# Turning the last group's probabilities on VectorE, and walking three column blocks of the output product side by side

## The chip, the cores and the metric

The kernel runs on one core of one Trainium2 chip. The metric is the device time of one execution in microseconds (us), as the median of the runs. Engines are named as in the profile: PE is TensorE's matmuls and PEld its weight loads, DVE is VectorE, ACT is ScalarE, POOL is GpSimd, SP is SyncE (here it only issues transfers).

## What is computed

Two layers on x (256 rows, 2048 columns, fp32). Each is x + rms_norm(mixer(rms_norm(x))). The change is in layer 0, whose mixer is attention:

```
proj = hn @ w_in                       # 256x2048 @ 2048x8192 -> q, k, v, z
q, k = rope(q), rope(k)                # 16 heads of 128
p = softmax(causal(q @ k.T * scale))   # one block of 256 keys: plain causal attention
y = ((p @ v) * silu(z)) @ w_out        # 256x2048 @ 2048x2048
```

Layer 1 is a gated depthwise convolution with a product on either side (w_in1, w_out1). Nothing in it is touched.

## The kernel before

**The large products.** Every product of 256 rows with a weight matrix is done in column blocks of 512 and slices of two k tiles of 128 (SL_K = 2, SLICES = 8 slices for K = 2048). fp32 accuracy comes from splitting both operands into a high and a low part in fp32r and adding three products: `slice_products` (L419) issues for each slice 2 k tiles x 2 row tiles x 3 parts = 12 matmuls of 128x128 with 128x512 (L429 to L431) into `acc[:, par, m]`. PSUM has eight banks: `acc` is two halves (par) of two banks (m = 0, 1), and `X[0]` to `X[3]` are four single banks for everything else.

**The weights' pipeline.** SyncE loads 1 MB (four k tiles, two slices) into one of four `raw` buffers (`load`, L299), and may do so when the low parts of the slices that were there before are made (`lo_ready`). ScalarE rounds a slice to its high part (`high`, L766, instruction L781) into one of four slots (RING = 4); for slice s it waits until TensorE has done slice s - 4 (`w_used`). VectorE subtracts to get the low part (`low`, L1057, instruction L1066), and TensorE waits for that (`lo_ready`) ahead of slice s. Each engine walks the same numbering of slices, and small work is put behind chosen slices of its own loop: `if s == ...` after `high(s)`, `low(s)` or `slice_products(s)`.

**Attention.** The first product (S_QKVZ) goes over four groups (G = 4 heads, 512 columns of q, k, v and z each; 32 slices a group). Behind slice 26 of a group TensorE makes the scores into `X[0..3]`; VectorE takes maxima and ScalarE exponentials (`exponentials`, L881), which end in `probs` (128 x 4 x 384: for each head three 128x128 blocks) and count `p_ready`. For the product with v the probabilities must be turned into `pT`.
- For groups 0 to 2 this happens in the next group's loop (`group_end`, L1186): VectorE turns 32x32 blocks from `probs` to `pT`, four instructions of 32x384 (`turn_probs`, L1165, instruction L1168) behind each of slices 2, 3, 4 and 5 (TURN_P = 2); TensorE multiplies with v behind slice 4 (`values`, L565; VALUES_AT = 4) into X[0] and X[1]; VectorE gates behind slice 7 (`gate_outputs`, L1132), turns the result behind slices 8 to 11 (`turn_heads`, L1179), and splits it behind 13 (`heads_low`, L1147), ScalarE making the high part behind its slice 13 (`heads_high`, L866).
- The last group's end lies in the output product's loop. There TensorE itself turns the probabilities behind slice 0: twelve transposes of 128x128 into X (`probs_T`, L559, instruction L562); VectorE copies them to `pT` behind slice 1 (`last_group_end`, L1198, instruction L1202), TensorE multiplies with v behind slice 1, and gating, turning and splitting follow behind slices 4, 5 to 8 and 10.

**The output product of layer 0** (S_OUT0, 32 slices, loop at L607). `OUT0_ORDER` (L76) names for every slice its column block n and its k slice. The last group's heads are k slices 6 and 7, and they are the last to be ready. So the order is block 0 slices 0 to 5, block 1 slices 0 to 5, then (0,6), (0,7), (1,6), (1,7), then blocks 2 and 3 whole. Block n accumulates in acc half n % 2. `ulo_ready` (L612) is the wait of TensorE for the split heads; `acc_free` (L451) is its wait, at a block's first slice, for the half to have been read.

**Emptying a block.** `OUT0_LAST` (L78) is the last slice of each block. Behind slices 17, 19 and 27 of their own loops ScalarE takes the squares of the rows of a block (`out0_squares`, L919; instruction L818, two instructions) and VectorE multiplies them with the gains to `y0` (`out0_rows`, L1247; instruction L1254, two instructions, counting `acc_read`). The gains `gpost0` are a 1 MB broadcast (L360), issued after the fourth load of the output weights, when TensorE has finished the last slice of the first product. The last four slices (28 to 31) are done for row tile 0 and then for row tile 1, and the next product's input is prepared between them.

Of the kernel before, what the change touches and what calls it, by code (L numbers as in the profile page):

```python
# [23 lines left out]
P = 128  # L24
# [50 lines left out]
SILU_AT = (1, 6)  # L75
OUT0_ORDER = tuple([(0, i) for i in range(6)] + [(1, i) for i in range(6)] + [(0, 6), (0, 7), (1, 6), (1, 7)]  # L76
                   + [(n, i) for n in (2, 3) for i in range(SLICES)])
OUT0_LAST = (13, 15, 23, 31)  # L78
TURN_Q, TURN_K = 15, 24
# [5 lines left out]
def build(nc, x, pre_g, post_g, w_in0, w_out0, w_in1, b_in, w_dw, b_dw, ln_g, ln_b, w_out1, b_out,  # L85
# [5 lines left out]
    with ctx:  # L91
# [126 lines left out]
        p_ready = sem("p_ready")  # L218
        pT_done = sem("pT_done")
        pT_ready = sem("pT_ready")  # L220
# [33 lines left out]
        row1_done = sem("row1_done")  # L254
        stored = sem("stored")

        block = ctx.enter_context(nc.Block())
# [148 lines left out]
        def _(pe):  # L406
# [11 lines left out]

            def slice_products(first, it, per, s, hi, lo, place=None):  # L419
                slot = s % RING  # L420
                block_no, part = place or (s // SLICES, s % SLICES)
                par = (first // SLICES + block_no) % 2
                pe.wait_ge(lo_ready[slot], rounds(first, it, per, s))
                order = [(i, m) for i in range(SL_K) for m in range(MT)]
                for n, (i, m) in enumerate(order):
                    k = SL_K * part + i
                    rows = slice(m * P, (m + 1) * P)
                    a = acc[:, par, m]
                    nc.tensor.matmul(a, hi[:, k, rows], w_hi[:, slot, i], start=(k == 0), stop=False)  # L429
                    nc.tensor.matmul(a, hi[:, k, rows], w_lo[:, slot, i], start=False, stop=False)  # L430
                    last = nc.tensor.matmul(a, lo[:, k, rows], w_hi[:, slot, i], start=False,  # L431
                                            stop=(k == KT - 1))
                last.then_inc(w_used[slot], 1)
# [124 lines left out]

            def probs_T(g, h):  # L559
                pe.wait_ge(p_ready, G * g + h + 1)  # L560
                for i in range(3):
                    last = nc.tensor.transpose(X[h][:, i * P:(i + 1) * P], probs[:, h, i * P:(i + 1) * P], ident[:])  # L562
                last.then_inc(pT_done, 1)

            def values(g):  # L565
# [41 lines left out]
            for s in range(4 * SLICES):  # L607
                n, part = OUT0_ORDER[s]
                if part == 0:
                    acc_free(16 + n)  # L610
                if n == 0 and part % 2 == 0:
                    pe.wait_ge(ulo_ready, part // 2 + 1)  # L612
                if s < 4 * SLICES - RING:
                    slice_products(S_OUT0, 0, 0, s, uT_hi, uT_lo, (n, part))
                if s == 0:
                    for h in range(G):
                        probs_T(NG - 1, h)
                if s == 1:
                    values(NG - 1)
# [145 lines left out]
        def _(act):  # L765
# [105 lines left out]

            def group_end(s, g, last=False):

                if s == 3:
                    if not (isinstance(g, int) and g == 0):
                        act.wait_ge(u_ready, g)
                    block_rows(S_QKVZ, g, 32, 31, z_row, rms[0], ACT.Silu)
                if s == (10 if last else SPLIT_U):
                    heads_high(g)
# [39 lines left out]
            def out0_squares(n):  # L919

                for m in range(MT):
                    if n == NG - 1 and m == 0:
                        act.wait_ge(row0_done, 1)
                    else:
                        act.wait_ge(w_used[OUT0_LAST[n] % RING], rounds(S_OUT0, 0, 0, OUT0_LAST[n]))
                    squares(junk1[:], acc[:, n % 2, m], m, n, 8 + MT * n + m)
                    if n == NG - 1 and m == 0:
# [5 lines left out]
            for s in range(4 * SLICES):  # L933
                high(S_OUT0, 0, 0, s)
                group_end(s, NG - 1, True)
                if s in (17, 19, 27):
                    out0_squares((17, 19, 27).index(s))
                if s > 4 * SLICES - RING:
# [117 lines left out]
        def _(dve):  # L1056
# [140 lines left out]

            def last_group_end(s):  # L1198
                if s == 1:
                    for h in range(G):  # L1200
                        dve.wait_ge(pT_done, h + 1)
                        nc.vector.tensor_copy(pT[:, h], X[h][:, 0:3 * P]).then_inc(pT_ready, 1)  # L1202
                    inverse_sums(NG - 1)
                if s == 4:
                    gate_outputs(NG - 1)
                if s in range(5, 9):
                    turn_heads(s - 5, NG - 1)
                if s == 10:
                    heads_low(NG - 1)

            def maxima(g, h):
# [35 lines left out]
            def out0_rows(n, ms=(0, 1)):  # L1247
# [3 lines left out]
                for m in ms:  # L1251
                    dve.wait_ge(ssq_ready, 8 + MT * n + m + 1)
                    c = slice(n * NCOL, (n + 1) * NCOL)
                    last = nc.vector.tensor_tensor(y0[:, m, c], acc[:, n % 2, m], gpost0[:, c], ALU.mult)  # L1254
                    if m == 1:
                        last.then_inc(acc_read, 1)

            for s in range(4 * SLICES):
                low(S_OUT0, 0, 0, s)
                last_group_end(s)  # L1260
                if s in (17, 19, 27):
                    out0_rows((17, 19, 27).index(s))
                if s > 4 * SLICES - RING:
# [339 lines left out]
```

## Time and profile before

| | |
|---|---|
| median of 3 runs | 845.37 us (845.22 to 845.59) |
| the profiled execution's own time | 845.41 us |
| span of the profiled execution | 843.6 us |
| mean granted TensorE clock | 0.998 |
| TensorE matmul busy | 833.9 us, 3851 instructions |
| VectorE busy | 703.9 us |
| ScalarE busy | 428.2 us |
| GpSimd busy | 341.2 us |

The span is from the first to the last instruction; the execution's time has 1.8 us around it. Times in the rows below are microseconds from the span's start, durations in us or ns as the row says. A matmul is shown from its start to its modelled end, and neighbours overlap: what one costs is the distance from its start to the next one's. A weight load (PEld) stands ahead of its matmul.

### The profile page before, as it was taken

The page shows a single profiled execution, that of the slowest core. Times are in us where ns is not written, and L with a number is a line of the kernel's source. Part 1 is how long each engine was busy: PE and PEld are TensorE (multiplying, and loading weights), DVE is VectorE, ACT ScalarE, POOL GpSimd, SP SyncE. Part 2 cuts the span into 40 slices and gives each one's busy share as a digit, 9 for nine tenths or more (in the row PEclk, how much of TensorE's full clock was granted, in tenths as well). Part 3 has the DMA queues.
Part 4 walks back from the last instruction along what each step waited for, and adds up shares of the span by engine and source line. Part 5 has one row for each costly group of instructions (what it writes and reads, how often), then busy time and mean ns, then how long its engine had stood idle before and what let it go on. Part 6 is the DMA issues. An engine that isn't in the chain of part 4 may idle for free.

```text
span 843.6 us, 12102 instructions
## 1 busy us (share of the span) xinstructions
PE 833.9 (99%) x3851; PEld 691.6 (82%) x3851; DVE 703.9 (83%) x1222; ACT 428.2 (51%) x592; POOL 341.2 (40%) x171
## 2 busy tenths in 40 slices
PE   9999999999999999999999999999999999999996
PEld 6888888888888888888888788888888888888884
DVE  5688799988999899968556629999999999998655
ACT  6744534464444635454445675445445464574541
POOL 0342005500540014400000298888888878894000
PEclk9999999999999999999999999999999999999999
DMA  9956556656567556646655466555555646566522
GB/s 316 315 169 206 175 157 193 198 158 197 156 188 220 177 149 183 215 149 223 216 186 192 133 200 200 176 176 197 188 167 193 198 151 200 194 219 244 192 99 100
DMA packets 97510, 159.50 MB, mean 189 GB/s; under 512 B 3300, under 2 KB 38468, under 8 KB 97092
## 3 DMA queue, kind: packets, MB, share of 16 engines
q1 hardware_dynamic: 97428, 159.04, 58.7%
q8 instruction: 20, 0.33, 0.2%
q14 instruction: 14, 0.11, 0.0%
q10 hardware_dynamic: 48, 0.02, 0.0%
HBM read 156.94 MB, written 2.10 MB: 189 GB/s over the span
## 4 chain that ended last, share of the span: by engine, by line
PE 98%; issue 1%; DMA 0%; DVE 0%; ACT 0%; DVEq 0%; POOLq 0%; POOL 0%; SPq 0%
PE acc L429 29%; PE acc L431 29%; PE acc L430 29%; PE X L439 1%; PE acc L414 1%; PE acc L416 1%; PE acc L415 1%; PE acc L495 1%; PE acc L510 1%; DMA xrow<-in_x 0%; PE X L571 0%; PE X L556 0%; PE X L555 0%; PE X L572 0%; PE X L570 0%
## 5 line engine op out<-in xcount | busy, mean ns | idle before, releaser
L781 ACT ACTIVATE w_hi<-raw 128x1024 fp32r<-128x1024 f32 x282 | 298.7, 1061 | 345.6 <-PE acc L431 345.0
L429 PE MATMUL acc<-w_hi,xT_hi 128*128 128x512 f32 x864 | 338.7, 392 | 0.0
L431 PE MATMUL acc<-w_hi,xT_lo 128*128 128x512 f32 x864 | 336.4, 389 | 0.0
L430 PE MATMUL acc<-w_lo,xT_hi 128*128 128x512 f32 x864 | 336.2, 389 | 0.0
L1066 DVE TENSOR_TENSOR w_lo<-raw,w_hi 128x1024 fp32r<-128x1024 f32 x180 | 242.1, 1362 | 72.3 <-ACT w_hi L781 70.0
L1550 POOL TENSOR_TENSOR w_lo<-raw,w_hi 128x1024 fp32r<-128x1024 f32 x102 | 248.0, 2438 | 48.8 <-ACT w_hi L781 48.4
L431 PEld LDWEIGHTS acc<-w_hi,xT_lo 128*128 128x128 f32 x864 | 162.2, 188 | 33.9
L429 PEld LDWEIGHTS acc<-w_hi,xT_hi 128*128 128x128 f32 x864 | 162.3, 188 | 33.2 <-DVE xT_lo L1085 0.3
L430 PEld LDWEIGHTS acc<-w_lo,xT_hi 128*128 128x128 f32 x864 | 162.3, 188 | 32.9
L1350 DVE SCALAR_TENSOR_TENSOR X<-u_pad,taps,X 128x256 f32<-128x256 f32 x464 | 182.6, 484 | 0.0
L1513 POOL TENSOR_TENSOR small<-small 128x1 f32<-128x1 f32 (+1 forms) x7 | 4.3, 617 | 222.9 <-DVE small L1296 124.2
L1527 POOL TENSOR_TENSOR rope_t<-q_row,sin_t 128x256 f32<-128x256 f32 x16 | 15.3, 988 | 178.8 <-ACT q_row L789 178.8
L429 PE MATMUL acc<-w_hi,uT_hi 128*128 128x512 f32 x112 | 43.8, 391 | 0.0
L429 PE MATMUL acc<-w_hi,vT_hi 128*128 128x512 f32 x112 | 43.7, 391 | 0.0
L431 PE MATMUL acc<-w_hi,vT_lo 128*128 128x512 f32 x112 | 43.6, 389 | 0.0
L431 PE MATMUL acc<-w_hi,uT_lo 128*128 128x512 f32 x112 | 43.6, 389 | 0.0
L430 PE MATMUL acc<-w_lo,vT_hi 128*128 128x512 f32 x112 | 43.6, 389 | 0.0
L430 PE MATMUL acc<-w_lo,uT_hi 128*128 128x512 f32 x112 | 43.6, 389 | 0.0
L1527 POOL TENSOR_TENSOR rope_t<-k_row,sin_t 128x256 f32<-128x256 f32 x16 | 16.2, 1042 | 44.3 <-ACT k_row L789 44.3
L1158 DVE STREAM_TRANSPOSE qT<-q_row 32x256 f32<-32x256 f32 x64 | 27.9, 436 | 1.0
L1158 DVE STREAM_TRANSPOSE kT<-k_row 32x256 f32<-32x256 f32 x64 | 27.9, 436 | 1.0
L1158 DVE STREAM_TRANSPOSE uT<-u_row 32x256 f32<-32x256 f32 x64 | 27.9, 436 | 1.0
(153 smaller groups left out, 770.7 us busy)
## 6 DMA issues: line engine op xcount, KB each, us to landing
raw<-in_w_in SPq DMA_DIRECT2D x78, 1024.0 KB, 5.3
raw<-in_w_in SPq DMA_DIRECT2D x66, 512.0 KB, 4.4
raw<-in_w_out SPq DMA_DIRECT2D x32, 1024.0 KB, 5.0
gpost<-in_post_g SPq DMA_DIRECT2D x2, 1024.0 KB, 6.4
xrow<-in_x SPq DMA_DIRECT2D x4, 256.0 KB, 5.8
raw<-in_w_in SPq DMA_DIRECT2D x4, 256.0 KB, 4.8
xrow<-in_x SPq DMA_DIRECT2D x2, 512.0 KB, 9.9
bout<-in_b_out SPq DMA_DIRECT2D x1, 1024.0 KB, 10.2
```

The costliest lines, as they stand in the source:

```text
L414: nc.tensor.matmul(a, hi[:, k, rows], wh[:, i], start=(k == 0), stop=False)
L415: nc.tensor.matmul(a, hi[:, k, rows], wl[:, i], start=False, stop=False)
L416: last = nc.tensor.matmul(a, lo[:, k, rows], wh[:, i], start=False, stop=(k == KT - 1))
L429: nc.tensor.matmul(a, hi[:, k, rows], w_hi[:, slot, i], start=(k == 0), stop=False)
L430: nc.tensor.matmul(a, hi[:, k, rows], w_lo[:, slot, i], start=False, stop=False)
L431: last = nc.tensor.matmul(a, lo[:, k, rows], w_hi[:, slot, i], start=False, stop=(k == KT - 1))
L781: nc.scalar.activation(w_hi[:, slot], raw[:, u % LOADS, 2 * half:2 * half + 2], ACT.Copy).then_inc(hi_ready[slot], 1)
L1066: nc.vector.tensor_tensor(lo_of(first, it, s), raw[:, u % LOADS, 2 * half:2 * half + 2], hi_of(first, it, s).bitcast(f32), ALU.subtract).t ...
L1158: last = nc.vector.transpose(dst[b * BLK:(b + 1) * BLK].rearrange("p h (m c) -> p m h c", m=MT) [:, :, :, a * BLK:(a + 1) * BLK], row[a * ...
L1350: ins = nc.vector.scalar_tensor_tensor(out=out_, in0=u, scalar=taps[:, bass.ds(tile + k * KT, 1)], in1=part, op0=ALU.mult, op1=ALU.add)
L1527: last = nc.gpsimd.tensor_tensor(t[:, :, o], v[:, :, w], sin_t[:, m:m + 1, o].to_broadcast([P, G, HALF]), ALU.mult)
L1550: nc.gpsimd.tensor_tensor(w_lo[:, slot], raw[:, u % LOADS, 2 * half:2 * half + 2], w_hi[:, slot].bitcast(f32), ALU.subtract).then_inc(lo_r ...
```

## The change

The last group is treated like the others: `probs_T`, its semaphore and `last_group_end` go, VectorE runs `group_end` in the output product's loop too, and TensorE multiplies with v behind slice 4. The last group's heads are so ready later, and the order of the output product is changed: three blocks go over k slices 0 to 5 (slices 0 to 17), then the same three over k slices 6 and 7 (slices 18 to 23), then block 3 whole (24 to 31). Three blocks open at a time need a third pair of banks: block 2 accumulates in X[2] and X[3] (`out0_bank`), and its first slice (12) waits for `p_ready` in place of `acc_free`. Blocks 0, 1 and 2 are emptied behind slices 23, 25 and 27.

```diff
--- before.py
+++ after.py
@@ -73,9 +73,10 @@
 OUT1_POOL = 10
 FINAL_AT = (0, 4, 8, 10)
 SILU_AT = (1, 6)
-OUT0_ORDER = tuple([(0, i) for i in range(6)] + [(1, i) for i in range(6)] + [(0, 6), (0, 7), (1, 6), (1, 7)]
-                   + [(n, i) for n in (2, 3) for i in range(SLICES)])
-OUT0_LAST = (13, 15, 23, 31)
+OUT0_ORDER = tuple([(n, i) for n in (0, 1, 2) for i in range(6)] + [(n, i) for n in (0, 1, 2) for i in (6, 7)]
+                   + [(3, i) for i in range(SLICES)])
+OUT0_LAST = (19, 21, 23, 31)
+OUT0_EVICT = (23, 25, 27)
 TURN_Q, TURN_K = 15, 24
 SCORES_AT = 26
 TURN_P, VALUES_AT, GATE_ROWS_AT, TURN_U, SPLIT_U = 2, 4, 7, 8, 13
@@ -216,7 +217,6 @@
         max_ready = sem("max_ready")
         negmax_ready = sem("negmax_ready")
         p_ready = sem("p_ready")
-        pT_done = sem("pT_done")
         pT_ready = sem("pT_ready")
         inv_ready = sem("inv_ready")
         pv_done = sem("pv_done")
@@ -254,6 +254,10 @@
         row1_done = sem("row1_done")
         stored = sem("stored")
 
+        def out0_bank(n, m):
+
+            return X[2 + m][:] if n == 2 else acc[:, n % 2, m]
+
         block = ctx.enter_context(nc.Block())
 
         def cols(w):
@@ -416,7 +420,7 @@
                     last = nc.tensor.matmul(a, lo[:, k, rows], wh[:, i], start=False, stop=(k == KT - 1))
                 return last
 
-            def slice_products(first, it, per, s, hi, lo, place=None):
+            def slice_products(first, it, per, s, hi, lo, place=None, banks=None):
                 slot = s % RING
                 block_no, part = place or (s // SLICES, s % SLICES)
                 par = (first // SLICES + block_no) % 2
@@ -425,7 +429,7 @@
                 for n, (i, m) in enumerate(order):
                     k = SL_K * part + i
                     rows = slice(m * P, (m + 1) * P)
-                    a = acc[:, par, m]
+                    a = banks[m][:] if banks else acc[:, par, m]
                     nc.tensor.matmul(a, hi[:, k, rows], w_hi[:, slot, i], start=(k == 0), stop=False)
                     nc.tensor.matmul(a, hi[:, k, rows], w_lo[:, slot, i], start=False, stop=False)
                     last = nc.tensor.matmul(a, lo[:, k, rows], w_hi[:, slot, i], start=False,
@@ -555,12 +559,6 @@
                 nc.tensor.matmul(s[:, 0:P], qT[:, h, 0:P], kT[:, h, 0:P], start=True, stop=True)
                 nc.tensor.matmul(s[:, 2 * P:3 * P], qT[:, h, P:SEQ], kT[:, h, P:SEQ], start=True, stop=True
                                  ).then_inc(s_done, 1)
-
-            def probs_T(g, h):
-                pe.wait_ge(p_ready, G * g + h + 1)
-                for i in range(3):
-                    last = nc.tensor.transpose(X[h][:, i * P:(i + 1) * P], probs[:, h, i * P:(i + 1) * P], ident[:])
-                last.then_inc(pT_done, 1)
 
             def values(g):
                 pe.wait_ge(pT_ready, G * (g + 1))
@@ -606,16 +604,15 @@
 
             for s in range(4 * SLICES):
                 n, part = OUT0_ORDER[s]
-                if part == 0:
+                if part == 0 and n == 2:
+                    pe.wait_ge(p_ready, G * NG)
+                elif part == 0:
                     acc_free(16 + n)
                 if n == 0 and part % 2 == 0:
                     pe.wait_ge(ulo_ready, part // 2 + 1)
                 if s < 4 * SLICES - RING:
-                    slice_products(S_OUT0, 0, 0, s, uT_hi, uT_lo, (n, part))
-                if s == 0:
-                    for h in range(G):
-                        probs_T(NG - 1, h)
-                if s == 1:
+                    slice_products(S_OUT0, 0, 0, s, uT_hi, uT_lo, (n, part), X[2:4] if n == 2 else None)
+                if s == VALUES_AT:
                     values(NG - 1)
 
             last_slices = range(4 * SLICES - RING, 4 * SLICES)
@@ -869,13 +866,13 @@
                     last = nc.scalar.activation(uT_hi[:, bass.ds(g * 4 + 2 * b, 2)], uT[:, 2 * b:2 * b + 2], ACT.Copy)
                 last.then_inc(uhi_ready, 1)
 
-            def group_end(s, g, last=False):
+            def group_end(s, g):
 
                 if s == 3:
                     if not (isinstance(g, int) and g == 0):
                         act.wait_ge(u_ready, g)
                     block_rows(S_QKVZ, g, 32, 31, z_row, rms[0], ACT.Silu)
-                if s == (10 if last else SPLIT_U):
+                if s == SPLIT_U:
                     heads_high(g)
 
             def exponentials(g, h, first):
@@ -923,7 +920,7 @@
                         act.wait_ge(row0_done, 1)
                     else:
                         act.wait_ge(w_used[OUT0_LAST[n] % RING], rounds(S_OUT0, 0, 0, OUT0_LAST[n]))
-                    squares(junk1[:], acc[:, n % 2, m], m, n, 8 + MT * n + m)
+                    squares(junk1[:], out0_bank(n, m), m, n, 8 + MT * n + m)
                     if n == NG - 1 and m == 0:
                         row_high(0, 0)
                         row_high(1, 0)
@@ -932,9 +929,9 @@
 
             for s in range(4 * SLICES):
                 high(S_OUT0, 0, 0, s)
-                group_end(s, NG - 1, True)
-                if s in (17, 19, 27):
-                    out0_squares((17, 19, 27).index(s))
+                group_end(s, NG - 1)
+                if s in OUT0_EVICT:
+                    out0_squares(OUT0_EVICT.index(s))
                 if s > 4 * SLICES - RING:
                     high(S_AG, 0, 16, s - (4 * SLICES - RING + 1))
             high(S_AG, 0, 16, RING - 1)
@@ -1195,19 +1192,6 @@
                 if s == SPLIT_U:
                     heads_low(g)
 
-            def last_group_end(s):
-                if s == 1:
-                    for h in range(G):
-                        dve.wait_ge(pT_done, h + 1)
-                        nc.vector.tensor_copy(pT[:, h], X[h][:, 0:3 * P]).then_inc(pT_ready, 1)
-                    inverse_sums(NG - 1)
-                if s == 4:
-                    gate_outputs(NG - 1)
-                if s in range(5, 9):
-                    turn_heads(s - 5, NG - 1)
-                if s == 10:
-                    heads_low(NG - 1)
-
             def maxima(g, h):
                 dve.wait_ge(s_done, G * g + h + 1)
 
@@ -1251,15 +1235,15 @@
                 for m in ms:
                     dve.wait_ge(ssq_ready, 8 + MT * n + m + 1)
                     c = slice(n * NCOL, (n + 1) * NCOL)
-                    last = nc.vector.tensor_tensor(y0[:, m, c], acc[:, n % 2, m], gpost0[:, c], ALU.mult)
+                    last = nc.vector.tensor_tensor(y0[:, m, c], out0_bank(n, m), gpost0[:, c], ALU.mult)
                     if m == 1:
                         last.then_inc(acc_read, 1)
 
             for s in range(4 * SLICES):
                 low(S_OUT0, 0, 0, s)
-                last_group_end(s)
-                if s in (17, 19, 27):
-                    out0_rows((17, 19, 27).index(s))
+                group_end(s, NG - 1)
+                if s in OUT0_EVICT:
+                    out0_rows(OUT0_EVICT.index(s))
                 if s > 4 * SLICES - RING:
                     low(S_AG, 0, 16, s - (4 * SLICES - RING + 1))
             low(S_AG, 0, 16, RING - 1)
```

## Rows read from the trace of the kernel before

**Rows 1.** The page, busy time by engine.
```profile
PE 833.9 (99%) x3851; PEld 691.6 (82%) x3851; DVE 703.9 (83%) x1222; ACT 428.2 (51%) x592; POOL 341.2 (40%) x171
```
**Rows 2.** Waits of TensorE, whole span: us in total, times, longest.
```profile
PE acc L537 <- POOL small L1508: 1.0, 1, 1.0
PE X L476 <- DMA xrow<-in_x: 0.3, 1, 0.3
```
**Rows 3.** Timeline of PE, output product's first seven slices: start, us, engine, line, operation.
```profile
378.61 0.39 PE L429 MATMUL acc<-w_hi,uT_hi 128*128 128x512 f32 x1
...
381.33 1.47 PE L562 MATMUL X<-ident,probs 128*128 128x128 f32 x12
382.56 0.48 PE L429 MATMUL acc<-w_hi,uT_hi 128*128 128x512 f32 x1
382.87 0.40 PE L430 MATMUL acc<-w_lo,uT_hi 128*128 128x512 f32 x1
...
385.41 0.38 PE L570 MATMUL X<-v_row,pT 128*128 128x128 f32 x2
...
396.27 0.39 PE L429 MATMUL acc<-w_hi,uT_hi 128*128 128x512 f32 x1
...
398.99 0.39 PE L429 MATMUL acc<-w_hi,uT_hi 128*128 128x512 f32 x1
```
**Rows 4.** Timeline of PE, the last group's own start: slices 0, 5 and 6.
```profile
286.18 0.39 PE L429 MATMUL acc<-w_hi,xT_hi 128*128 128x512 f32 x1
...
302.38 0.48 PE L429 MATMUL acc<-w_hi,xT_hi 128*128 128x512 f32 x1
...
305.19 0.39 PE L429 MATMUL acc<-w_hi,xT_hi 128*128 128x512 f32 x1
```
**Rows 5.** Timelines of DVE and PEld at that border, then at the first.
```profile
284.81 1.23 DVE L1066 TENSOR_TENSOR w_lo<-raw,w_hi 128x1024 fp32r<-128x1024 f32 x1 [1.49 <-ACT w_hi L781]
...
288.36 1.23 DVE L1066 TENSOR_TENSOR w_lo<-raw,w_hi 128x1024 fp32r<-128x1024 f32 x1
...
291.96 1.23 DVE L1066 TENSOR_TENSOR w_lo<-raw,w_hi 128x1024 fp32r<-128x1024 f32 x1
...
296.82 2.33 DVE L1168 STREAM_TRANSPOSE pT<-probs 32x384 f32<-32x384 f32 x4
...
299.56 0.41 PEld L570 LDWEIGHTS X<-v_row,pT 128*128 128x128 f32 x2
...
111.97 2.33 DVE L1168 STREAM_TRANSPOSE pT<-probs 32x384 f32<-32x384 f32 x4
...
114.70 0.41 PEld L570 LDWEIGHTS X<-v_row,pT 128*128 128x128 f32 x2
```
**Rows 6.** Both kinds of turning by source line: ns min/median/max, first and last start.
```profile
L562 PE MATMUL X<-ident,probs x12: 270/272/273, 381.3 to 382.5; 128*128 128x128 f32 x12
L1168 DVE STREAM_TRANSPOSE pT<-probs x48: 514/570/574, 101.2 to 298.6; 32x384 f32<-32x384 f32 x48
```
**Rows 7.** Stretches: length; busy by engine PE, PEld, DVE, ACT, POOL; PEclk, DMA share, GB/s.
```profile
381.33:385.41 4.08, 4.08 (x25) 3.57 (x24) 3.55 (x7) 2.12 (x3) 0.00 (x0) 1.00 0.98 388
286.18:302.38 16.20, 16.20 (x86) 13.86 (x84) 14.99 (x21) 8.80 (x9) 0.00 (x0) 1.00 0.57 176
```
**Rows 8.** Timelines of ACT, SP and DVE around the start of the output product.
```profile
372.15 0.20 ACT L887 ACTIVATION_READ_ACCUMULATOR probs<-X,small 128x1 f32 x1
...
378.80 0.34 SPq L360 DMA_DIRECT2D gpost<-in_post_g  x1
...
381.86 1.95 DVE L1202 COPY pT<-X 128x384 f32<-128x384 f32 x4 [6.12 <-PE X L562]
...
383.83 3.45 DVE L1066 TENSOR_TENSOR w_lo<-raw,w_hi 128x1024 fp32r<-128x1024 f32 x3
```
**Rows 9.** Timelines of DVE and PE: the first block read, and slice 16.
```profile
423.24 1.28 DVE L1254 TENSOR_TENSOR y<-acc,gpost 128x512 f32<-128x512 f32 x2
...
426.19 0.39 PE L429 MATMUL acc<-w_hi,uT_hi 128*128 128x512 f32 x1
```

## The prediction

> **What bounds the kernel now.** I read the page first: TensorE is busy for 99% of the span [rows 1], and the chain of waits below it on the page runs through TensorE nearly throughout. So a change is worth what it does to TensorE's stream, unless it makes TensorE wait. The list of waits says the same more sharply: in the whole span TensorE waited for another engine twice, for 1.0 and 0.3 us, both in the first microseconds [rows 2]. Busy time alone is not enough, since matmuls overlap; I therefore went on to the timeline, where the cost of an instruction is the distance between the starts of its neighbours. A slice of the weights is twelve matmuls, and one slice to the next is 2.72 us (396.27 to 398.99 [rows 3]), so 0.2267 us per matmul although each is shown as 0.39 us long.
>
> The place of the change is the start of the first output product, at 378.61 [rows 3]. There the reader should see two interruptions: twelve transposes of the probabilities behind slice 0, and the products with the values behind slice 1. The other three groups of heads have the same work in the other form, turned by VectorE, and the values behind slice 4; the border between the third and the last group is the model for what the changed kernel will do [rows 4, 5].
>
> **The twelve transposes go.** Their mean is 272 ns [rows 6], but they lie in each other: the first starts at 381.33 and the next product at 382.56, so the path holds 1.23 us for them, 0.103 us each. Behind them slice 1 runs from 382.56 to 385.41, 2.85 us in place of 2.72: 0.13 us more, of which 0.08 is the first matmul (next start after 0.31, not 0.23) and the rest small excesses in the same slice [rows 3]. Sum: 1.23 + 0.13 = 1.36 us. A second way to the same number: the first slice's start to the sixth slice's start holds five slices and the values at either border. It is 378.61 to 396.27 = 17.66 with transposes and values after slice 1 [rows 3]. At the model border 286.18 to 302.38 is 16.20, up to the restart after the values, whose own excess then falls into the next slice (302.38 to 305.19, 2.81, so 0.09) [rows 4]. 17.66 - 16.20 - 0.09 = 1.37. I take 1.36. The ends: 1.23 if the slow slice has another cause (it lay under transfers that kept the queues 98% busy [rows 7]), and 1.37.
>
> **A rule on the price of a transpose.** The trace shows 272 ns as duration and 0.103 us as distance. The Trainium skill (TensorE: Matmul & The Clock Gate, Part 4: PE-mode transpose) gives about 275 ns for a 128x128 transpose in a kernel's context; the duration in the trace agrees, and by the rule taken as a price per transpose the saving would be more than twice as large.
>
> **The copies go, turns come.** VectorE loses four copies (1.95 us from 381.86 [rows 8]) and the 6.12 us that it waited for TensorE before them. It gains sixteen block transposes, four per slice over slices 2 to 5, 2.33 us for the last four at the model border [rows 5], 16 x 0.57 = 9.1 us in all by the median of one [rows 6]; so it is some 7.2 us busier. Nothing of this lies on TensorE's path as long as the last turn ends before the values need it. That is the one new wait that can matter, and I price it from the model: VectorE works there without a pause from 284.81 to 299.15 (four splits, a reciprocal, sixteen turns; 14.34 us), and TensorE loads the first turned block at 299.56 [rows 5]. The cover is 0.41 us. At the border of the first two groups it is the same: 111.97 + 2.33 = 114.30 against 114.70 [rows 5]. Slice 0 starts at 378.61, which is 92.43 us after 286.18 [rows 3, 4], and what ScalarE does for slices 2 to 5 is the same at both borders, so the chain should run from 377.24 to 391.58 and the values start their load at 391.99. The probabilities themselves are finished at 372.15 + 0.20 = 372.35 [rows 8], long before. Cost: 0, with 0.41 us in hand; behind a late turn TensorE would simply stand, with slice 5 queued behind the values.
>
> Could the turns be slower here than in the model? The one thing that is different is traffic: the 1 MB broadcast of the gains is issued at 378.80, and the queues are 98% busy from 381.33 to 385.41, against 57% at the model border [rows 7, 8]. Three splits inside that traffic took 3.45 us, 1.15 each, no more than the 1.23 of the model border [rows 5, 8]. So I take nothing. The Trainium skill (SBUF, State Buffer; section SBUF: two separate sides) says that a transfer and a compute operation cannot slow each other there; by this the reserve stays whole, and the splits under traffic agree.
>
> The Trainium skill (VectorE: DVE Perf Modes, Rules for kernel authors) also speaks against the change: for a 128x128 transpose it recommends TensorE. By cost per engine the trace agrees, 9.1 us on VectorE against 1.23 on TensorE, but what counts here is which engine has time to spare.
>
> **Gate, turning and splitting of the last heads move later** (slices 7, 8 to 11 and 13 instead of 4, 5 to 8 and 10; ScalarE's part from 10 to 13). TensorE needs the result for the last four row tiles, now first in slice 18 instead of slice 12. By the model's spacing slice 18 starts near 378.61 + 2.60 + 18 x 2.72 + 0.1 = 430.3. The heads' split follows slice 13's low part, whose high part waits for slice 9, done near 408.5; three VectorE steps of some 3 us later it is there, near 415. Cost 0, about 15 us in hand. The loads of the weights keep their sizes and number, only their addresses swap; SyncE's queue waits for the low parts, which come at the model's times. Cost 0.
>
> **The third block in two other banks.** Ninety-six matmuls write X2 and X3 in place of acc. No row has this form; from above I bound it by the excess of a restart, 0.08 us [rows 3], at each of the four changes of block, 0.3 us. A gain is excluded, since the pitch is 0.2267 us in every block already. Nearest are the alternating banks m = 0 and 1 inside a slice, which cost nothing: 0. Its wait for p_ready is long met in slice 12.
>
> **Emptying the blocks** moves from slices 17, 19, 27 to 23, 25, 27; the first two keep their distance of four slices behind the block's last product. What is new: block 3 reuses the second half of acc in slice 24, two slices after the second block ends in slice 21. Before, the first block had the same distance (last product in slice 13, next use in slice 16): read by 423.24 + 1.28 = 424.52, needed at 426.19, 1.67 us in hand [rows 9]. Cost 0. Behind a late reading slice 24 and all the rest would stand.
>
> **Sum.** -1.36 us. The profiled execution took 845.41 us around a span of 843.6 and is 0.04 above the median of 845.37. So 845.41 - 1.36 = 844.05 for it, span 842.2, and 844.0 for the median: 0.16% less. A measurement of this kernel can tell about 0.2%, 1.69 us, from no change, so the likeliest outcome counts as no change though the direction is down.
>
> **Rivals.**
> First, the transposes cost their whole duration: 12 x 0.272 = 3.26 us, so 842.1, faster. For it: 272 ns in the row [rows 6]. Against it: 1.23 us between their neighbours [rows 3]. Chance 0.04. (This is what the page's 275 ns would give.) With 0.08 for a smaller surplus, over 0.33 us beyond my sum, from restarts that I have missed: faster 0.12.
> Second, the turns come somewhat late, by 0.4 to 1.7 us, and eat the gain: around 844.9. Against: three borders of groups, and no wait at any [rows 2]. Chance 0.07, counted as no change.
> Third, ending slower: the same wait, but one whole step of VectorE (split and turn, 3.60 us, 288.36 to 291.96 [rows 5]) later. TensorE stands 3.60 - 0.41 = 3.19 us in front of the values, net +1.83, 847.2. It decides once the last turn is over 0.41 + 1.36 + 1.69 = 3.46 us late. For it: the thin cover and a chain without a pause. Against: the same alignment as the model, and splits that do not slow under traffic. Chance 0.05.
> Fourth, the second block is read a slice late: 2.72 - 1.67 = 1.05 us lost in front of slice 24, 845.1, no change. Chance 0.02.
> That leaves 0.74 for the forecast itself, and no change in all 0.83.
>
> **Range.** The forecast's own spread is 843.7 to 844.4 (terms 1.23 to 1.37, 0.3 for the banks, and 0.2 for the scatter of the runs). Towards the late turns I go to 845.1, and below to 843.5 for part of the surplus. What is outside is the whole-duration case, the slower one and the tails.
>
> **What would show it.** The row of transposes and copies is gone; 64 block turns of the probabilities instead of 48; no interruption behind slice 0; the values' load about 13.4 us after the start of slice 0; TensorE's waits still only two; five slices with values 16.2 us. Wrong: a wait of TensorE for the turns or for the reading of acc, or a pitch over 0.227 us in the third block.

## The result, and the profile after

| | before | changed |
|---|---|---|
| median | 845.37 us | 848.46 us (846.68 to 848.79, 7 runs) |
| profiled execution | 845.41 us | 846.72 us |
| its span | 843.6 us | 844.9 us |

The ratio over all runs is 1.0027, 95% interval [1.0017, 1.0037]: 0.27% slower, where 844.0 and no measurable change were forecast. The seven runs fall into two heaps, three at 846.68 to 847.26 with a mean granted clock of 0.997 and four at 848.46 to 848.79 with 0.995. The median lies in the upper heap, so the medians are further apart, 3.1 us or 0.37%; the profiled execution is of the lower heap.

At the place of the change everything went as forecast. The timeline of PE in the changed kernel, at the first slice, at the values and at the sixth slice:

```profile
378.48 0.39 PE L433 MATMUL acc<-w_hi,uT_hi 128*128 128x512 f32 x1
...
392.08 0.38 PE L568 MATMUL X<-v_row,pT 128*128 128x128 f32 x2
...
394.68 0.48 PE L433 MATMUL acc<-w_hi,uT_hi 128*128 128x512 f32 x1
```

Slice 0 to slice 5 is 394.68 - 378.48 = 16.20 us, as at the model border [rows 4], against 17.66 before [rows 3]. The last turn and the load of the first turned block, from the timelines of DVE and PEld:

```profile
389.13 2.33 DVE L1165 STREAM_TRANSPOSE pT<-probs 32x384 f32<-32x384 f32 x4
...
391.86 0.41 PEld L568 LDWEIGHTS X<-v_row,pT 128*128 128x128 f32 x2
```

389.13 + 2.33 = 391.46, so 0.40 us in hand; 0.41 was forecast. The loss lies some 350 us further on. The waits of TensorE in the changed kernel, which answer to [rows 2]:

```profile
PE acc L433 <- issue: 2.1, 1, 2.1
PE acc L541 <- POOL small L1492: 1.0, 1, 1.0
PE X L706 <- POOL small L1497: 0.4, 1, 0.4
```

Two are new. The big one is ahead of the last product of layer 1 (`vT_hi`). The profile puts it down to "issue", but the program has TensorE wait there for the low part of `vT`, which VectorE makes. The small one (L706) is ahead of the matmuls that spread the statistics of the convolution's rows, some 20 us earlier, and these start from sums that VectorE makes too. The profile's chain tells whose lateness it is:

```profile
PE 70%; DVE 16%; issue 9%; DVEq 3%; ACT 1%; DMA 0%; POOL 0%; POOLq 0%; SPq 0%; ACTq 0%
PE acc L433 20%; PE acc L435 20%; PE acc L434 20%; DVE X L1334 12%; DVEq L1333 2%; DVE u_pad L1345 2%; PE acc L418 1%; PE acc L420 1%; PE acc L419 1%; PE X L433 1%; PE X L435 1%; PE X L434 1%; PE acc L514 1%; PE acc L499 1%; PE X L443 1%
```

VectorE had 0% of this chain before, and TensorE 98%. L1334 are the convolution's taps and L1345 is the gate of a pair of its input tiles (u_pad times sigmoid). VectorE walks eight pairs, each with one gate and 62 taps, from the first sigmoid to the statistics that the last product needs. Timelines around the start of the last product, first of the kernel before and then of the changed one:

```profile
743.70 3.42 DVE L1424 TENSOR_TENSOR vT_lo<-cT,vT_hi 128x1024 fp32r<-128x1024 f32 x1
...
746.96 0.39 PE L431 MATMUL acc<-w_hi,xT_lo 128*128 128x512 f32 x1
747.23 0.47 PE L429 MATMUL acc<-w_hi,vT_hi 128*128 128x512 f32 x1
```

```profile
745.07 3.40 DVE L1408 TENSOR_TENSOR vT_lo<-cT,vT_hi 128x1024 fp32r<-128x1024 f32 x1
...
746.11 0.39 PE L435 MATMUL acc<-w_hi,xT_lo 128*128 128x512 f32 x1
748.57 0.47 PE L433 MATMUL acc<-w_hi,vT_hi 128*128 128x512 f32 x1 [2.07 <-issue]
```

Before, VectorE's low part ended at 743.70 + 3.42 = 747.12 and TensorE started at 747.23, 0.04 us behind its usual pitch: both chains arrived together, and nothing of this wait was long enough to be listed. Afterwards TensorE is there 0.85 us earlier (746.11) and VectorE 1.35 us later (748.47). The distance to the next start is 2.46 us (746.11 to 748.57) where it was 0.27, so 2.19 more. The sum is -0.85 + 2.19 = +1.34 us, the 1.3 us between the spans. Ahead of the statistics TensorE had been 1.46 us early (728.25 against 729.71); the other 0.61 us went into the small wait.

VectorE starts the convolution 1.47 us earlier (the first gates below) and comes out of it 2.37 us later. The first instruction behind it, from the timelines of DVE before and after:

```profile
716.57 3.66 DVE L1378 BATCH_NORM_STATS2 small<-c_row 128x6 f32<-128x512 f32 x6
```

```profile
718.94 3.65 DVE L1362 BATCH_NORM_STATS2 small<-c_row 128x6 f32<-128x512 f32 x6
```

The loop is thus 3.84 us longer. Up to the last product 1.0 of the 2.37 us are made good: before, VectorE had waited 0.38 us for TensorE on the way, and one of its products (L1413, now L1397) had taken 3.03 us in place of 2.40. Where the convolution loses its time is seen in the eight gates. Timeline of DVE, the first four gates before:

```profile
505.94 0.69 DVE L1361 TENSOR_TENSOR u_pad<-u_pad,sig  x1 [10.96 <-ACT sig L983]
...
531.82 0.69 DVE L1361 TENSOR_TENSOR u_pad<-u_pad,sig  x1 [0.26 <-issue]
...
557.49 2.64 DVE L1361 TENSOR_TENSOR u_pad<-u_pad,sig  x1 [0.23 <-issue]
...
585.11 0.69 DVE L1361 TENSOR_TENSOR u_pad<-u_pad,sig  x1 [0.23 <-issue]
```

and after:

```profile
504.47 0.69 DVE L1345 TENSOR_TENSOR u_pad<-u_pad,sig  x1 [10.94 <-ACT sig L980]
...
530.47 2.85 DVE L1345 TENSOR_TENSOR u_pad<-u_pad,sig  x1 [0.28 <-issue]
...
558.34 0.69 DVE L1345 TENSOR_TENSOR u_pad<-u_pad,sig  x1 [0.27 <-issue]
...
584.05 2.77 DVE L1345 TENSOR_TENSOR u_pad<-u_pad,sig  x1 [0.27 <-issue]
```

A gate takes 0.69 us or up to 2.9 us, and the eight are 0.69, 0.69, 2.64, 0.69, 2.90, 0.69, 0.69, 1.74 before (10.73 us) and 0.69, 2.85, 0.69, 2.77, 0.69, 2.78, 1.28, 2.63 after (14.38 us): 3.65 us more, out of the 3.84. In this stretch GpSimd splits the weights, 2.40 us in each 2.72, so that a gate nearly always meets a split. The splits nearest to the second gate, before and then after:

```profile
531.84 7.84 POOL L1550 TENSOR_TENSOR w_lo<-raw,w_hi 128x1024 fp32r<-128x1024 f32 x3 [0.32 <-ACT w_hi L781]
```

```profile
530.37 2.40 POOL L1534 TENSOR_TENSOR w_lo<-raw,w_hi 128x1024 fp32r<-128x1024 f32 x1 [0.31 <-ACT w_hi L778]
```

Before, the gate (531.82) starts 0.02 us ahead of the split and is undisturbed. After, it starts (530.47) 0.10 us behind the split and ends at 533.32, 0.55 us after the split's end. My theory (A): a gate that starts behind a split of GpSimd waits for its end, and a few hundredths of a microsecond decide which of the two is first; from then on all later gates fall otherwise. The Trainium skill (SBUF, State Buffer; section SBUF: two separate sides) describes it: a VectorE operation with two SBUF inputs and a GpSimd operation that reads SBUF need a shared pair of ports, whoever starts first has it for the whole instruction, "the other fully blocks". The gate has two SBUF inputs, and both traces agree in both directions. The eight gates in them that start while a split runs all end 0.55 us behind that split's end. A split that starts while a gate runs is lengthened in its turn; beside the sixth gate of the kernel before (638.67 to 639.36) it takes 2.78 us in place of 2.40:

```profile
638.84 2.78 POOL L1550 TENSOR_TENSOR w_lo<-raw,w_hi 128x1024 fp32r<-128x1024 f32 x1 [0.39 <-ACT w_hi L781]
```

The rivals: (B) the loss comes from the output product's new order or its banks; (C) VectorE's convolution loop is slower apart from its gates (by the two profiles it is, but only by 0.19 us); (D) it is TensorE's earlier arrival that sets how gates and splits meet.

### The profile page after: what moved, and what is told of

Its sections match the earlier page's. It is cut to its first block, busy times and chain, and to the rows that moved or that the text cites. A ratio compares the mean times of both kernels' runs of the same rounds, so it can differ in the third digit from the quotient of the medians.

```text
span 844.9 us, 12090 instructions
## 1 busy us (share of the span) xinstructions
PE 833.0 (99%) x3839; PEld 690.1 (82%) x3839; DVE 714.0 (85%) x1234; ACT 428.0 (51%) x592; POOL 341.3 (40%) x171
## 4 chain that ended last, share of the span: by engine, by line
PE 70%; DVE 16%; issue 9%; DVEq 3%; ACT 1%; DMA 0%; POOL 0%; POOLq 0%; SPq 0%; ACTq 0%
PE acc L433 20%; PE acc L435 20%; PE acc L434 20%; DVE X L1334 12%; DVEq L1333 2%; DVE u_pad L1345 2%; PE acc L418 1%; PE acc L420 1%; PE acc L419 1%; PE X L433 1%; PE X L435 1%; PE X L434 1%; PE acc L514 1%; PE acc L499 1%; PE X L443 1%
## 5 line engine op out<-in xcount | busy, mean ns | idle before, releaser
L1334 DVE SCALAR_TENSOR_TENSOR X<-u_pad,taps,X 128x256 f32<-128x256 f32 x464 | 182.7, 482 | 0.0
L1165 DVE STREAM_TRANSPOSE pT<-probs 32x384 f32<-32x384 f32 x64 | 36.3, 567 | 1.0
L433 PE MATMUL acc<-w_hi,uT_hi 128*128 128x512 f32 x80 | 31.2, 390 | 0.0
L434 PE MATMUL acc<-w_lo,uT_hi 128*128 128x512 f32 x80 | 31.1, 389 | 0.0
L435 PE MATMUL acc<-w_hi,uT_lo 128*128 128x512 f32 x80 | 31.1, 389 | 0.0
```

Source lines behind the costliest of these rows:

```text
L1165: last = nc.vector.transpose(pT[b * BLK:(b + 1) * BLK].rearrange("p h (i c) -> p (h i) c", i=3) [:, :, a * BLK:(a + 1) * BLK], probs[a * B ...
L1334: ins = nc.vector.scalar_tensor_tensor(out=out_, in0=u, scalar=taps[:, bass.ds(tile + k * KT, 1)], in1=part, op0=ALU.mult, op1=ALU.add)
```

## Experiments

The number that a measured time is set against is the median of the kernel before in the same comparison. Unless said otherwise, the outputs are computed in full.

**The sigmoid in a PSUM bank, loop unrolled.** X[3] is free during the convolution and X[1] between its transposes; the gate then has one SBUF input.

```diff
-last = nc.scalar.activation(sig[:, buf, c], X[1][...], ACT.Sigmoid, ...)
+last = nc.scalar.activation(X[3 - 2 * buf][...], X[1][...], ACT.Sigmoid, ...)
-with dve.Fori(0, SLICES) as h:
-    nc.vector.tensor_tensor(pair, pair, sig[:, bass.ds(h % 2, 1)]..., ALU.mult)
+with dve.Fori(0, SLICES // 2) as q:
+    for b in (0, 1):
+        h = q * 2 + b
+        nc.vector.tensor_tensor(pair, pair, X[3 - 2 * b]..., ALU.mult)
# and TensorE waits for gate h - 1 before it writes X[1] for an even pair h
```

On the changed kernel:

> The changed kernel, but ScalarE puts the sigmoid into a PSUM bank (X[3] for even, X[1] for odd pairs), so that VectorE's gate of the convolution input has one SBUF input instead of two. Theory A (the gates were held up by GpSimd's low-part splits): all eight gates take about 0.7 us, the end of the convolution on VectorE comes 8 to 9 us earlier, TensorE does not wait ahead of the last product, and the local saving of 1.36 us is seen in full: 844.0. Theory B (the loss is in the output product's new order, the third pair of banks or the emptying): the loss stays, 846.5 to 848.5. Theory C (VectorE's convolution loop itself is slower in the changed kernel, gates aside): most of the loss stays, over 846.

On the kernel before:

> The same edit on the kernel before. Theory A: its gates lose about 5 us of delay too, but TensorE waited there by 0.1 us at most, so the median stays near 845.3, and the difference to the changed kernel with this edit is the 1.36 us of the transposes. Theories B and C: near 845.3 as well, with the changed kernel above it.

Measured: 849.11 us and 850.2 us against 845.06, ratios 1.0044 [1.0031, 1.0058] and 1.0048 [1.0034, 1.0062]. Both forecasts missed, by the time. The timeline of DVE of the first shows why; gates 2 to 4:

```profile
530.67 0.68 DVE L1350 TENSOR_TENSOR u_pad<-u_pad,X 128x512 f32 x1
...
559.30 0.69 DVE L1350 TENSOR_TENSOR u_pad<-u_pad,X 128x512 f32 x1 [2.98 <-issue]
...
585.00 0.68 DVE L1350 TENSOR_TENSOR u_pad<-u_pad,X 128x512 f32 x1
```

All eight gates are 0.68 or 0.69 us, as theory A has it. But at each of the three turns of the now twice as long loop VectorE stands for 2.98, 2.83 and 4.42 us with nothing to wait for in the program, and TensorE waits 3.2 us for the sixth gate. So the edit had a cost of its own, and this pair decides nothing about the total. I took the length of the loop's body as the cause of the pauses, and tested that below.

**A nudge of 0.1 us, on the kernel before.**

```diff
+if first:
+    nc.scalar.activation(small[:, 120:121], rms[2][:, 0:1], ACT.Copy)   # one column, not used
 for c in range(2):
     nc.scalar.activation(u_pad[...], X[0][...], ACT.Identity, ...)
```

> The kernel before with one ScalarE copy of one column ahead of the very first sigmoid, so that VectorE's convolution starts some 0.1 to 0.3 us later against GpSimd's splits and nothing else changes. Theory A: the second gate, which in the kernel before starts 0.02 us ahead of a split, now starts behind it and takes over 2 us; other gates fall differently too, TensorE waits ahead of the last product and the median is 1 to 3 us above before, about 847. Theories B and C: at most 0.3 us above before, 845.4 to 845.7.

Measured: 849.4 us (848.11 to 849.75) against 845.06, ratio 1.0047 [1.0033, 1.0061]. From the transposes ahead of it to the first gate it is 4.61 us (501.16 to 505.77) instead of 4.51 (501.43 to 505.94). The second gate and the split beside it:

```profile
531.65 2.87 DVE L1363 TENSOR_TENSOR u_pad<-u_pad,sig  x1 [0.26 <-issue]
```

```profile
531.57 2.40 POOL L1552 TENSOR_TENSOR w_lo<-raw,w_hi 128x1024 fp32r<-128x1024 f32 x1 [0.32 <-ACT w_hi L781]
```

0.10 us more, and the gate is 0.08 us behind the split. The eight gates are then those of the changed kernel within 0.1 us (2.87, 2.85, 2.87, 1.30 and 2.69 in the same places), and TensorE waits 2.0 us for VectorE. This is theory A in the kernel before, with nothing of the change in it; B and C allow 0.3 us. The size was larger than the 1 to 3 us that I gave: the profiled execution, 848.11, is 3.05 us above, and the median 4.3. What lies between these two no trace of this run shows.

**TensorE's twelve transposes put back into the changed kernel**, result not used:

```diff
+if s == 0:
+    pe.wait_ge(p_ready, G * NG)
+    for h in range(G):
+        for i in range(3):
+            nc.tensor.transpose(X[h][:, i * P:(i + 1) * P], probs[:, h, i * P:(i + 1) * P], ident[:])
```

> The changed kernel with the twelve TensorE transposes of the probabilities put back behind slice 0 (their result is not used). All the rest is as changed. Theory A with the program's layout or a small delay on VectorE deciding the race, not TensorE's earlier arrival: the gates are held up as in the changed kernel and the time is 1.2 to 1.5 us above it, 848 to 850. Theory D (it is TensorE's earlier arrival by 1.36 us that sets the phase): the gates fall as in the kernel before and the time is 845.4.

Measured: 849.14 us against 845.06. The gates are 0.69, 2.86, 0.69, 2.77, 0.69, 2.78, 1.27, 2.63, as in the changed kernel. D falls: with TensorE's work as before, VectorE is still late. Here the profile caught something more. Stretches of this kernel: the wait ahead of the last product, the ten matmuls behind it, and the next ones:

```profile
747.10:749.50 2.40, 0.38 (x2) 0.00 (x0) 2.37 (x2) 2.40 (x5) 1.49 (x2) 1.00 0.02 7
749.53:753.26 3.73, 3.73 (x10) 2.91 (x11) 3.51 (x9) 1.75 (x3) 3.73 (x2) 0.54 0.78 279
753.30:757.00 3.70, 3.70 (x20) 3.06 (x19) 3.67 (x3) 2.08 (x3) 2.35 (x2) 1.00 0.45 127
```

(length; busy by PE, PEld, DVE, ACT, POOL; PEclk, DMA share, GB/s.) After the wait of about 2 us the granted clock is 0.54, so nearly all of the stretch is at 1.2 GHz instead of 2.4; the tenth start behind it comes 3.75 us after the first instead of 2.12, which is 1.6 us. In the changed kernel's profile the same wait did not bring the clock down (the matmuls behind 748.57 keep their pitch). That fits the two heaps of its runs, 2.0 us apart with mean clocks of 0.997 and 0.995. Of the changed kernel itself no slower run was profiled. The nearest is the changed kernel with six idle instructions (below, profiled at 848.63 us and 0.995), whose gates are the same to 0.01 us. Behind its wait the granted clock is down too, with matmuls 0.43 us apart, again 1.6 us in all:

```profile
748.85:752.30 3.45, 3.45 (x10) 2.68 (x11) 3.33 (x8) 1.73 (x3) 3.45 (x2) 0.59 0.96 300
```

So the upper heap is most likely the lower one with this half clock added, 1.6 of the 2.0 us.

**The sigmoid in a bank, loop not unrolled.** X[0] to X[3] become slices of one PSUM tensor XX, so that the gate can choose its bank by an index; the loop body keeps its length.

```diff
+X = [XX[:, i] for i in (2, 1, 3, 0)]
-nc.vector.tensor_tensor(pair, pair, sig[:, bass.ds(h % 2, 1)]..., ALU.mult)
+nc.vector.tensor_tensor(pair, pair, XX[:, bass.ds(h % 2, 1)]..., ALU.mult)
# ScalarE's sigmoid and TensorE's two waits for the gates as in the first edit
```

> The changed kernel with the sigmoid in a PSUM bank and the gate with one SBUF input, but VectorE's loop over the pairs not unrolled this time: the bank is chosen by an index, so the loop body is as long as in the changed kernel. Theory A (gates held up by GpSimd's splits): no gate over 0.75 us, no pause of 2.6 to 4.4 us at the loop's turn, the convolution ends 8 us earlier than in the changed kernel (near 708 instead of 716.6), TensorE does not wait ahead of the last product: 844.0. If the pauses of the unrolled loop had another cause than its length (the bank, the waits of TensorE), they stay and the time is over 848.

> The same edit on the kernel before. Theory A: 845.3, no more than 0.1 us of TensorE's waits to gain, and 1.36 us above the changed kernel with the edit. Otherwise over 848.

Measured against 845.28: the changed kernel with it 844.37 us, ratio 0.9989 [0.998, 0.9998]; the kernel before with it 845.54, ratio 1.0003 [0.9994, 1.0012]. Two lines of the first's timeline of DVE:

```profile
684.75 0.69 DVE L1349 TENSOR_TENSOR u_pad<-u_pad,X  x1 [0.27 <-issue]
...
722.82 1.30 DVE L1366 BATCH_NORM_STATS2 small<-X 128x6 f32<-128x512 f32 x2 [5.44 <-PE X L701]
```

The last gate begins at 684.75 (691.64 in the changed kernel), all eight take 0.69 us, no turn of the loop over 0.28, and VectorE now waits 5.44 us for TensorE ahead of the last statistics. It comes out of the convolution at 710.11, 8.8 us earlier than in the changed kernel (the "708 instead of 716.6" of my expectation used the time of the kernel before for the comparison). TensorE's wait ahead of the last product is gone. So: with the collisions away the changed kernel is 1.17 us faster than the kernel before with the same edit, where 1.36 was forecast. By the two ratios it is 1.2 us, and their intervals just overlap, so this size is rough. It is also 4.1 us below the changed kernel's own median, from another comparison. The pauses of the unrolled loop went with its length, while the bank and TensorE's new waits stayed.

**The two parts apart, both with the gate in a bank.** Order, banks and emptying alone (turning as before, by TensorE):

> With the gate in a bank, so that the convolution does not cover what is measured: the new order, the third pair of banks and the later emptying alone; the probabilities are turned by TensorE and copied by VectorE as before. Theory A: this part costs and brings nothing, 845.3. Theory B (order or banks cost): above 845.6.

Turning alone (the output product's old order, `OUT0_EVICT` 17, 19, 27):

> With the gate in a bank: VectorE turns the probabilities, but the output product keeps the order of the kernel before, so that TensorE needs the last group's split heads in slice 12. In the changed kernel's trace they are there at 412.8 and slice 12 starts at 413.8, so TensorE should just not wait: 844.0 if it holds, up to 845.0 if the split is late by a microsecond.

Measured against 845.28: order alone 845.24 us, ratio 1.0004 [0.9995, 1.0013]; turning alone 843.95 us, ratio 0.9985 [0.9976, 0.9994]. B falls. TensorE waits nowhere in the output product in either. Turning alone has the lowest median of the study, clear of the kernel before, but the 0.4 us to the whole change with the gate in a bank are within the noise. The split heads are in time for slice 12, so the third pair of banks is not needed.

**What made the gate late: the length of VectorE's program.** In the changed kernel the first round of the loop is 26.00 us (504.47 to 530.47) against 25.88 before, and each turn of it 0.27 instead of 0.23. In both kernels the split beside the second gate starts 25.90 us behind the first gate (505.94 to 531.84, 504.47 to 530.37), so it is the length of this round, 25.88 or 26.00, that puts the gate ahead of it or behind. VectorE has twelve instructions more ahead of the loop. The two parts apart point the same way: order alone, without the twelve, has rounds of 25.87 and turns of 0.23, turning alone, with them, 26.00 and 0.27. Twelve or six fills of one column, put where VectorE waits 11 us for the first sigmoid:

```diff
+for i in range(12):
+    nc.vector.memset(small[:, 112 + i:113 + i], 0.0)
 with dve.Fori(0, SLICES) as h:
```

> The kernel before with twelve one-column fills on VectorE ahead of the convolution loop, in the 11 us in which VectorE waits there for the first sigmoid: the program is as many instructions longer as the changed kernel's. Theory L (the place of VectorE's loop in its program decides how long a round takes): the first round takes 26.00 us instead of 25.88, the turn of the loop 0.27 instead of 0.23, the second gate falls behind a split and the median is 848 to 850. If it is the block turns themselves or their data, not the length, rounds stay at 25.88 and the median at 845.3.

> The same with six fills. Theory L: either of the two patterns, and the time goes with it: with a turn of 0.23 us 845.3, with 0.27 us 848 to 850.

> The changed kernel with six such fills. Theory L: either of the two patterns; if the turn of the loop is 0.23 us and the first round 25.88, the second gate starts ahead of the split as in the kernel before, gates fall as there and the time is 844.0 to 844.5; if it stays at 0.27 us, 846.7 to 848.7.

Measured against 845.3: twelve on the kernel before 848.96 us, 1.0036 [1.0022, 1.0051]; six 848.4, 1.0036 [1.0021, 1.005]; six on the changed kernel 847.83, 1.0025 [1.0016, 1.0035]. The second gate of the first:

```profile
532.11 2.85 DVE L1363 TENSOR_TENSOR u_pad<-u_pad,sig  x1 [0.28 <-issue]
```

It starts 26.00 us behind the first (506.11), and the eight gates are those of the changed kernel to 0.01 us. So the kernel before becomes as slow as the changed one by instructions that do nothing and cost nothing where they stand. Six do the same (26.11 us, turns of 0.27), and on the changed kernel six leave the rounds and the gates as they are. That a longer program lengthens the loop's first round and its turns is shown; by what rule of place it does so is open, and six was the only other length tried on the changed kernel.

## Why the prediction was wrong

- **The transposes, -1.36 us: right.** Five slices with the values take 16.20 us, and with the collisions away the two kernels are 1.17 us apart (turning alone against the kernel before with the bank: 1.59). The forecast's own spread was added up wrongly: the terms named, 0.13 and 0.3 upwards and 0.2 either way, give 843.8 to 844.6 and not 843.7 to 844.4; nothing hangs on it.
- **The turns on VectorE, cost 0 with 0.41 us in hand: right**, 0.40 us. So was what the Trainium skill (SBUF, State Buffer; section SBUF: two separate sides) says of transfers and compute operations: VectorE's chain took 14.35 us (377.11 to 391.46) against 14.34 at the model border, with the queues 99% busy from 381 to 385. The recommendation of the Trainium skill (VectorE: DVE Perf Modes, Rules for kernel authors) to turn on TensorE would have cost here.
- **Heads, order, banks, emptying, cost 0: right**, 845.24 alone, against 845.28 for the kernel before and 845.54 for it with the gate in a bank. The pitch in the third block stayed at 2.72 us a slice, and the second block was read 1.66 us ahead of slice 24, where 1.67 was forecast.
- **The step that failed is the first one**, "a change is worth what it does to TensorE's stream, unless it makes TensorE wait", with the list of waits as its proof. A list without waits says that no other engine was late; it does not say by how much they were early. Ahead of the last product VectorE was early by nothing (747.12 against 747.23), and I looked for reserve only where the change stands. A gain on TensorE could there be kept only if the convolution moved along as a whole.
- **It did not move along**, because its length hangs on a race: 0.02 us decided that the kernel before took 10.7 us for its gates and not 14.4. The change made VectorE's program longer, the first round 0.12 us longer and the race lost: 3.65 us more for the gates and 0.19 for the rest of the loop, less 1.47 us of earlier start, make the statistics 2.37 us late. On TensorE that is 0.6 us at the statistics and 2.2 us ahead of the last product, of which the earlier start had paid 1.46. Four of the seven runs take 2 us more; that in these the clock fell behind the wait is inferred from their mean clock and from the trace of the kernel nearest to them.
- **The rival for "slower" had the wrong place.** I put it at the values, with 0.05; the real one was a wait that the change does not touch. That its 847.2 lies between the two heaps of the measured runs is luck. The range, 843.5 to 845.1, had no room for a second chain of equal length.

## What to carry to other kernels

An engine that never waits may still have a second chain right behind it: before costing a gain, look at every later meeting point for how early the other side was, not only for listed waits. Where VectorE operations with two SBUF inputs run beside GpSimd operations, their time is a draw and not a number; one operand in PSUM brought the eight gates from 10.7 or 14.4 us down to 5.5, and a comparison of two versions is only clean once such draws are taken out. A nudge of 0.1 us, or idle instructions, tells quickly whether a kernel's time rests on such a draw.

## What the runs showed that I had not expected

- Six to twelve instructions ahead of a loop lengthened each turn of it from 0.23 to 0.27 us and its first round by 0.12 us or more.
- A VectorE loop of two pairs (some 126 instructions) paused for 2.6 to 4.6 us at each turn; the loop of one pair (some 63) did not.
- A wait of about 2 us on TensorE was followed by half the clock in some executions and not in others: of six profiles with this wait (2.0 to 2.1 us of idle time each) three have matmuls 0.43 us apart behind it (transposes put back, six fills on either kernel), and three keep their pitch (the changed kernel, the nudge, twelve fills). The granted clock was 0.54 over 3.7 us in one of the first kind, and 1.00 in the changed kernel.
- The slower variants of the kernel before (849.4, 848.96, 848.4) cost 3 to 4 us for a shift of 0.1 to 0.2 us.
